# Moving VectorE work between convolution taps, earlier weight loads for six projections, and other places for 9 expert chunks

## The reference, cut

```python
for i in range(DEPTH):                                   # first block
    h = rmsnorm(x, mix_norm[i]) * (1.0 + sc1) + sh1
    y = fox_mixer(h, ...) if i % 2 == 0 else mla_mixer(h, ...)   # w_in, attention, w_out
    x = x + g1 * y
    h = rmsnorm(x, ffn_norm[i]) * (1.0 + sc2) + sh2
    x = x + g2 * hier_moe(h, ...)
...
h = adaln(x, shift1, scale1)                             # second block
p = h @ w_in                                             # 1024 columns for the convolution, 1792 for RWKV
u = p_conv[..., :512] * jax.nn.sigmoid(p_conv[..., 512:])
u = lax.conv_general_dilated(u, conv_w, ..., feature_group_count=512) + conv_b    # 31 taps, causal
y_conv = jax.nn.silu(layer_norm(u, conv_ln_g, conv_ln_b))
p_prev = jnp.pad(p_rw[:, :-1], ((0, 0), (1, 0), (0, 0)))
xm = p_rw + (p_prev - p_rw) * mu_shift                   # "mix": this token's and the one before
...                                                      # rwkv7_scan of r, k, v, decay, a, gate
y1 = jnp.concatenate([y_conv, y_rw], axis=-1) @ w_out
x = layer_norm(ALPHA * x + gate1 * y1, ln1_g, ln1_b)
...
sc, ci = lax.top_k(cand, PEER_TOPK)                      # 8 heads x 16 of 16384 experts per token
z = jnp.einsum('td,tkd->tk', hb, u_sel)
act = jax.nn.gelu(z, approximate=False) * gb
y2 = jnp.einsum('tk,tkd->td', act, jnp.take(peer_v, eb, axis=0))
```

## Time and profile before

| | |
|---|---|
| three runs | 3748.47, 3749.78, 3760.42 us (median 3749.78) |
| profiled execution | 3751.27 us, of which the span is 3749.5 |
| granted TensorE clock, mean | 0.898 |
| busy: PE, DVE, ACT, POOL | 81%, 65%, 34%, 25% |
| DMA | 704.64 MB, 188 GB/s on average |

### The profile page before, as it was taken

How to read it: one execution, slowest core, us unless ns; L and a number is a source line. 1 busy time by engine, 2 the same in 40 slices (tenths; PEclk the granted TensorE clock), 3 DMA queues, 4 the chain that set the end, 5 groups by cost and what they waited for, 6 DMA issues and landing times. The chain is left out here.

```text
span 3749.5 us, 45482 instructions
## 1 busy us (share of the span) xinstructions
PE 3023.0 (81%) x15603; PEld 2456.2 (66%) x15603; DVE 2435.1 (65%) x4011; ACT 1288.5 (34%) x2145; POOL 921.4 (25%) x629
## 2 busy tenths in 40 slices
PE   6989869976886999646378464886798999999995
PEld 2886656646666666334256353686788888888884
DVE  1767766546777654563623556887775777777777
ACT  1325434434551443114101012254453333333332
POOL 0001100210120012082012011364563344333331
PEclk8999979988988999777589686998899999999998
DMA  4861459944027896211000011225567888888884
GB/s 171 302 238 31 166 223 364 362 169 173 6 85 259 331 353 263 79 45 43 15 15 1 6 62 62 74 85 159 167 198 261 313 309 326 326 323 320 326 327 180
DMA packets 229813, 704.64 MB, mean 188 GB/s; under 512 B 30084, under 2 KB 109060, under 8 KB 210836
## 3 DMA queue, kind: packets, MB, share of 16 engines
q1 hardware_dynamic: 182712, 481.31, 35.5%
q0 software_dynamic: 46944, 221.27, 16.2%
HBM read 645.32 MB, written 57.18 MB: 187 GB/s over the span
## 5 line engine op out<-in xcount | busy, mean ns | idle before, releaser
L455 PE MATMUL peer_chunks_low<-peer_chunks_down_hi,peer_chunks_bent_hi 128*128 128x512 f32 x768 | 300.1, 391 | 3.8 <-DVE peer_chunks_bent_lo L2830 3.6
L457 PE MATMUL peer_chunks_low<-peer_chunks_down_hi,peer_chunks_bent_lo 128*128 128x512 f32 x768 | 300.6, 391 | 0.0
L456 PE MATMUL peer_chunks_low<-peer_chunks_down_lo,peer_chunks_bent_hi 128*128 128x512 f32 x768 | 300.4, 391 | 0.0
L2704 POOL DMA_INDIRECT peer_chunks_got_up<-in_peer_u_rows,peer_rows_at x128 | 203.4, 1589 | 290.7 <-DVE peer_chunks_got_up L2834 279.8
L455 PE MATMUL peer_chunks_risen<-peer_h_hi,peer_chunks_up_hi 128*128 128x384 f32 x640 | 216.3, 338 | 4.9 <-DVE peer_chunks_up_lo L2811 4.7
L457 PE MATMUL peer_chunks_risen<-peer_h_hi,peer_chunks_up_lo 128*128 128x384 f32 x640 | 215.9, 337 | 0.0
L456 PE MATMUL peer_chunks_risen<-peer_h_lo,peer_chunks_up_hi 128*128 128x384 f32 x640 | 215.3, 336 | 0.0
L2710 POOL DMA_INDIRECT peer_chunks_got_down<-in_peer_v,peer_rows_at x128 | 132.7, 1037 | 257.6 <-DVE mod L2846 251.2
L455 PEld LDWEIGHTS peer_chunks_low<-peer_chunks_down_hi,peer_chunks_bent_hi 128*128 128x128 f32 x768 | 144.4, 188 | 35.6 <-issue 7.6
L2846 DVE SCALAR_TENSOR_TENSOR mod<-peer_chunks_got_down,peer_chunks_shares,mod 128x1024 f32<-128x1024 f32 x128 | 163.9, 1280 | 4.3 <-DVE peer_chunks_shares L2839 1.2
L2811 DVE TENSOR_TENSOR peer_chunks_up_lo<-hT,peer_chunks_up_hi 128x1024 fp32r<-128x1024 f32 x80 | 97.9, 1224 | 104.2 <-ACT peer_chunks_up_hi L2763 102.9
(11 more groups left out here) (675 smaller groups left out, 8661.8 us busy)
## 6 DMA issues: line engine op xcount, KB each, us to landing
moe_raw<-in_moe_gate_up SPq DMA_DIRECT2D x32, 2048.0 KB, 9.2
hT<-in_peer_v SPq DMA_DIRECT2D x128, 512.0 KB
hT<-in_peer_u SPq DMA_DIRECT2D x112, 512.0 KB, 4.4
fox_o<-in_side_w SPq DMA_DIRECT2D x80, 512.0 KB, 5.7
peer_w<-peer_ahead_stage SPq DMA_DIRECT2D x24, 1024.0 KB, 7.1
peer_chunks_weights<-peer_w SPq DMA_DIRECT2D x128, 192.0 KB
mla_o<-in_side_w SPq DMA_DIRECT2D x40, 512.0 KB, 5.3
moe_raw_dn<-in_moe_down SPq DMA_DIRECT2D x16, 1024.0 KB, 8.7
```

What stands on the lines that cost most here:

```text
L455: nc.tensor.matmul(out, l_hi, r_hi, start=start, stop=False)
L456: nc.tensor.matmul(out, l_hi, r_lo, start=False, stop=False)
L457: return nc.tensor.matmul(out, l_lo, r_hi, start=False, stop=stop)
L2704: pool.indirect_dma_start(got_up[:, c % GOT], None, a["peer_u_rows"], bass.IndirectOffsetOnAxis(ap=rows_at[:, c:c + 1], axis=0)).then_inc( ...
```

## The change

1. **hybrid_in.** POOL has no work any more. DVE makes the 14 cuts and the 14 mixes between steps of the convolution: 52 steps (`AHEAD_STEPS`) first, then 14 times a cut, 5 steps (`STEPS`) and the mix of the chunk before. The mix reads PE's sum from PSUM, and ACT's copy `earlier` is gone. The steps go channel after channel, so each waits for the one before it. The weights have three slots in place of two.
2. **Projections.** A new class `EarlyWeights` loads the first two pieces in the stage ahead (fox_norm, fox_attn, mla_norm, mla_latents, mla_attn, and rwkv's last stage), behind that stage's own loads of gains. Piece 0 is rounded and cut in halves, the first ahead of the left side, the second in its middle. Chunk 0 runs slice by slice, with the transposes of slices 4 to 7 between, and `LateRows` and the gate logits come after it.
3. **peer_ahead.** `AT_PICK` goes from (8, 7, 7) to (11, 10, 10); `REST` falls from 14 to 5 and takes its stores over 5 moves.
4. Some scratch buffers (mla's squares and rotation parts, hybrid_out's late sums) lie in buffers that exist anyway, to make room.

The diff, cut to its core:

```diff
@@ hybrid_in @@
+    PAD, CONV_CHUNKS, SLOTS, RAWS = TAPS - 1, 2 * CC, 2, RAW_CHUNKS
+    AHEAD_STEPS, STEPS = 52, 5
...
             def _(pe):
                 for n in range(IN_CHUNKS):
-                    if n >= SLOTS:
+                    if n >= CONV_CHUNKS + SLOTS:
+                        pe.wait_ge(mixed, n - CONV_CHUNKS - SLOTS + 1)
+                    elif n >= SLOTS:
                         pe.wait_ge(kept, n - SLOTS + 1)
...
-            @block.gpsimd
-            def _(pool):
-                def split(n):
-                    pool.wait_ge(w_rounded, n - CONV_CHUNKS + 1)
-                    nc.gpsimd.tensor_tensor(w_lo[:, n % SLOTS], raw[:, n % SLOTS], w_hi[:, n % SLOTS].bitcast(F32), ALU.subtract).then_inc(w_split, 1)
...
             @block.vector
-                    for j in range(TAPS):
-                        for c in range(first, first + PAIR):
...
-                                dve.wait_ge(tapped, TAPS * first + PAIR * (j - 1) + c - first + 1)
...
+                def tap(c, j):
+                    if j == 0:
                         dve.wait_ge(kept, 2 * c + 2)
                         v.tensor_tensor(u[:, c, PAD:], pT[:, c], bent[:, c], ALU.mult).then_inc(gated, 1)
+                        dve.wait_ge(gated, c + 1)
+                        v.tensor_scalar(out[:, c], u[:, c, :SEQ], w[:, c, 0:1], b[:, c:c + 1], ALU.mult, ALU.add).then_inc(tapped, 1)
+                    else:
+                        dve.wait_ge(tapped, TAPS * c + j)
+                        v.scalar_tensor_tensor(out[:, c], u[:, c, j:j + SEQ], w[:, c, j:j + 1], out[:, c],
+                                               ALU.mult, ALU.add).then_inc(tapped, 1)
...
+                def split(m):
+                    slot, place = (CONV_CHUNKS + m) % SLOTS, (CONV_CHUNKS + m) % RAWS
+                    dve.wait_ge(w_rounded, m + 1)
+                    v.tensor_tensor(w_lo[:, slot], raw[:, place], w_hi[:, slot].bitcast(F32), ALU.subtract).then_inc(w_split, 1)
+
+                def mix(m):
+                    at = CONV_CHUNKS + m
+                    dve.wait_ge(weighed, m + 1)
+                    v.scalar_tensor_tensor(pT[:, at, 1:], acc[:, at % SLOTS, :SEQ - 1], mu[:, m:m + 1], pT[:, at, 1:],
+                                           ALU.mult, ALU.add).then_inc(mixed, 1)
...
+                taps(0, AHEAD_STEPS)
+                for m in range(MIXED):
+                    split(m)
+                    taps(AHEAD_STEPS + STEPS * m, STEPS)
+                    if m:
+                        mix(m - 1)
+                taps(AHEAD_STEPS + STEPS * MIXED, CC * TAPS)
+                mix(MIXED - 1)
@@ EarlyWeights and project_rows @@
+class EarlyWeights:
+    def __init__(self, nc, name, pieces, raw):
+        self.pieces, self.raw, self.sems = pieces, raw, ExitStack()
+        self.w_in = [self.sems.enter_context(nc.semaphore(f"{name}_w_in{u}")) for u in range(2)]
+
+    def load(self, sp):
+        for n in range(2):
+            sp.dma_start(piece_place(self.raw, self.pieces, n), self.pieces[n].w).then_inc(self.w_in[n], 16)
...
+    FIRST = len(pieces[0].ks) // 2
...
                 for n in range(chunks):
                     if n + 2 < chunks:
-                        sp.wait_ge(w_split, n + 1)
+                        sp.wait_ge(w_split, n + 2)
                         sp.dma_start(of(raw, n + 2), pieces[n + 2].w).then_inc(w_in[n % 2], 16)
+                    if n == 0 and rows is not None:
+                        sp.wait_ge(turned, kc)
...
+                for j, k in enumerate(pieces[0].ks):
+                    pe.wait_ge(w_split, 1 if j < FIRST else 2)
+                    pe.wait_ge(l_split, k + 1)
+                    for t in range(TILES):
+                        product(0, t, j, k)
+                    if rows is not None and k + TILES < kc:
+                        turn(k + TILES)
+                for e in extras:
+                    e.tensor(pe, 0)
...
+                round_(0, slice(FIRST))
                 for k in range(kc):
+                    if k == FIRST:
+                        round_(0, slice(FIRST, None))
                     if rows is not None:
                         act.wait_ge(turned, k + 1)
                     nc.scalar.copy(l_hi[:, k], left(k)).then_inc(l_rounded, 1)
-                for n in range(2):
-                    round_(n)
+                round_(1)
...
@@ fox; the same in mla and hybrid @@
-                                                          LateRows(nc, s, g, a["side_b"], 0, g.next, [acc[:, 1, 2], acc[:, 1, 3]], at=-1)])
+                                                          LateRows(nc, s, g, a["side_b"], 0, g.next, [acc[:, 1, 2], acc[:, 1, 3]])])
@@ peer_ahead @@
-    AT_PICK, AT_TURN, AT_GROUPS, EXP_AT, RING, LATER, BY_ACT, RAWS = (8, 7, 7), 2, 4, 4, 3, 3, 4, 3
+    AT_PICK, AT_TURN, AT_GROUPS, EXP_AT, RING, LATER, BY_ACT, RAWS = (11, 10, 10), 2, 4, 4, 3, 3, 4, 3
...
                 for j, m in enumerate(REST):
-                    move(m, TILES - 1, range(j, j + 1) if j < STORES else ())
+                    move(m, TILES - 1, range(j * STORES // len(REST), (j + 1) * STORES // len(REST)))
```

176 lines of the change are left out of this document (87 added, 89 removed).

## The result

The changed kernel takes 3647.78 us (median of 4 runs, 3640.07 to 3652.17) against 3752.88 of the kernel before in the same series: ratio 0.9716, 95% interval 0.9692 to 0.974. A second series of five gave 0.9712 (0.9694 to 0.9729). That is 2.8% faster (2.9% in the second series); 3650 us was predicted. The profiled execution is the fastest of its series, 3640.07 (span 3638.3), so by the two profiles the kernel gained 111.2 us and by the medians 105.

A forecast was written before the change was run, and what follows sets the result against it. TensorE is busy 81% of the span and stages run one after another behind barriers, so what ends last bounds each. Gains of 47+10+9+5+2.3+3.5+1+24 = 101.8 off 3751.27 give 3649.5, predicted as 3650 us; range 3630 to 3682.

The forecast's parts named there:

- The stall was VectorE against GpSimd: hybrid_in: GpSimd's 34.90 us subtraction waits for the port VectorE holds; this goes once GpSimd has no work there.
- a dependent tap: hybrid_in, VectorE: a tap that waits for the one before it costs 0.78 us, bounds 0.66 and 0.86.
- Rival A: hybrid_in: taps keep 0.66 us, stage gains 55, total 3642, or 3632 if side sums follow; chance 0.17.
- the late rows under chunk 0: fox_out, hybrid_out: what GpSimd makes for the late rows lies under chunk 0; fox_out gains 10 us, hybrid_out 9.
- only the cuts move up: a third of fox_out's 10: mla_out: side loads still wait for all transposes, so only VectorE's weight cuts come earlier; gain 3.5 us (1 to 10).
- its bounds: fox_in: gain between −4 and 6.8 us; the lower bound is side sums shifted by gate logits behind chunk 0.
- The tail: peer_ahead: lifts after VectorE's end, 28.97 us idle until the barrier; nine fewer lifts give 26 us.
- ACT's wait for the stores goes, 11 us in all: peer_ahead: ACT's 6.17 us wait for stores and its like in the next part vanish, 11 us in all.
- The central case: Whole kernel: the time lands between 3642 and 3662 us; chance 0.50.
- B: Rival: VectorE or stores take more in peer_ahead, hybrid_in and projections; total 3665, 3675 or 3690 us; chance 0.28.
- C: Rival: kernel gets slower through hybrid_in's taps one after another, from 1.60 us a tap; chance 0.02.
- D: Rival: early weights hidden where DMA or side sums end projection stages; 31 us falls to 3, total 3678; part of B.

## Why the prediction was right, and where it wasn't

In brackets stand the gain predicted and the gain measured, in us.

**hybrid_in (47; 49.3).** Every step held. The stall was VectorE against GpSimd, a dependent tap costs 0.79 us, and the first product came at 1571.11, where the sum with the stage's shift of 27.6 gives 1570.4. The 2 us more are the rounds, 5.60 and not 5.74: the next instruction starts 0.66 behind a mix and 1.13 behind a cut. Rival A (taps keep 0.66) is refuted in the changed kernel; its price, 55 us, is confirmed in the run that alternates (135.3, 54.6 less than before). The Trainium skill's rule ("VectorE: DVE Perf Modes", section "The DRAIN you can't avoid") that chaining by semaphores costs nothing extra doesn't carry over to this instruction. Every tap waits for a semaphore in either order; the taps start 0.67 us apart where the wait is for the tap before last and 0.79 where it is for the last.

**fox_out, hybrid_out, mla_up, mla_in (26.3; 28.7).** The sizes held. One step was incomplete. The prediction put the late rows under chunk 0 and left it at that, but what GpSimd makes for them was itself late, by 5 us, through loads behind the weights' own DMAs. With the early loads and the old order the first product of fox_out comes 15.7 us into the stage, where it came at 23.4. In the stretch with fox_out the order alone gives 7.8 us, the early loads alone 9.0 and both 12.6: the two overlap, and either would have brought most of it. I hadn't counted that.

**mla_out (3.5; 6.9).** The step "only the cuts move up: a third of fox_out's 10" failed. The last weight cut starts 47.9 us into the stage (1126.32 less 1078.45) and stood at 55.4 (1155.33 less 1099.93). VectorE's work wasn't a closed chain: before the change the third cut waited for ScalarE's rounding, and ScalarE waited for TensorE's chunks, 21.5 us in two waits. So TensorE's earlier start reached the end by two thirds.

**fox_in (1; −1.2).** It lies inside its bounds, but the loss is twice what I had put down for it, 4 us, for the gate logits behind chunk 0. They cost 8 (190.5 against 182.4), because they stop VectorE, VectorE stops SP's side loads, and those stand ahead of the weights' loads. Without that the early pieces would have gained 7.

**peer_ahead (24; 22.4).** The tail went as forecast (25.4 of 26 us). VectorE's end came 3.0 us later, where 2 was predicted, but by other terms, and that is luck. The first group's masks came 10.1 us later in the stage (12.5 predicted). "ACT's wait for the stores goes, 11 us in all" failed: the waits fell from 6.2 and 5.9 to 4.4 and 3.9, so 3.8 us went and not 11. The DMA engines are full from 2470 to 2510 (share 1.08, 330 GB/s), when the loads of lifts meet the eight stores of 1 MB; that this keeps the waits up is my reading and wasn't tested. What gave time back instead was the last pick, 4.1 us shorter, because with 5 lifts in the rest no GpSimd subtraction lies beside its two multiplications. The second and the third pick together lost as much: in each, one multiplication went from 2.29 to 4.36 beside the added lifts. I had neither of these terms. VectorE's lag behind the kernel before was 10.2 us at the second pick, 9.4 at the third, 7.2 at the last and 3.0 at its end.

**The whole.** The central case held; the prices of B and C were not paid. D (early weights hidden where something else ends the stage) was taken for fox_in, mla_in and mla_out. In fox_in the number came out so, but what hid the 7 us were the gate logits; mla_in and mla_out gained as much as forecast or more. That the time came within 3 us of 3650 is partly luck. By the profiles the kernel gained 111 us and not 102: mla_out, hybrid_in and the small projections gave 8 us more, fox_in and peer_ahead 4 less, and 5 came from stages that weren't counted. The median of the changed kernel lies 8 us above its profiled execution, which covers the difference.
